# Keeping the residual as token rows: the norms behind the first FFN and the second out-projection done per chunk of 128 tokens

## The reference, cut to what matters

```python
def rmsnorm(x, g):
    y = xf * lax.rsqrt(jnp.mean(xf * xf, axis=-1, keepdims=True) + EPS)
    return (y * g.astype(F32)).astype(x.dtype)
...
x <- x + gate * RMSNorm_post(f(RMSNorm_pre(x) * (1 + scale) + shift))
```

## Time and profile before

| | us |
|---|---|
| median of 3 runs | 1950.3 (1949.1 to 1951.3) |
| the profiled execution, its own time | 1951.7 |
| its span in the profile | 1949.9 |
| PE busy | 1896.0 (97%) |
| VectorE busy | 987.0 (51%) |
| ScalarE busy | 666.7 (34%) |
| GpSimd busy | 191.5 (10%) |

### The profile page before, as it was taken

How to read it: one execution, slowest core, us unless ns; L and a number is a source line. 1 busy time by engine, 2 the same in 40 slices (tenths; PEclk the granted TensorE clock), 3 DMA queues, 4 the chain that set the end, 5 groups by cost and what they waited for, 6 DMA issues and landing times.

```text
span 1949.9 us, 29286 instructions
## 1 busy us (share of the span) xinstructions
PE 1896.0 (97%) x11961; PEld 1742.5 (89%) x11961; DVE 987.0 (51%) x1763; ACT 666.7 (34%) x869; POOL 191.5 (10%) x172
## 2 busy tenths in 40 slices
PE   6999999989999999999999999999999999999998
PEld 5768987759999999998999999998898998899987
DVE  5415446476553555558543343336367653355533
ACT  4323234343331333335422223224344432133312
POOL 3100001410000000141000000001240000000002
PEclk8999999999999999999999999999999999999999
DMA  9843103762213231344232221335753221323221
GB/s 276 337 173 98 55 28 116 243 203 65 78 54 96 74 86 51 89 134 157 84 103 67 92 79 38 101 110 186 246 130 87 78 73 54 97 65 86 65 86 55
DMA packets 243851, 214.36 MB, mean 110 GB/s; under 512 B 7804, under 2 KB 227188, under 8 KB 238644
## 3 DMA queue, kind: packets, MB, share of 16 engines
q1 hardware_dynamic: 234163, 193.45, 32.9%
q10 hardware_dynamic: 7504, 10.74, 1.6%
q0 software_dynamic: 2096, 8.94, 1.3%
HBM read 197.89 MB, written 11.02 MB: 107 GB/s over the span
## 4 chain that ended last, share of the span: by engine, by line
PE 83%; DVE 9%; issue 2%; DMA 2%; ACT 2%; POOL 1%; SPq 0%; DVEq 0%; POOLq 0%; ACTq 0%
PE PJ L2141 43%; PE PJ L2304 8%; PE PJ L2152 7%; PE AT L2610 4%; PE PJ L2610 3%; PE PJ L2275 2%; PE AT L2162 2%; PE AT L2491 1%; DVE uT L1406 1%; PE AT L2507 1%; DMA xT<-in_ada_w 1%; PE AT L2120 1%; PE PJ L2162 1%; PE AT L2504 1%; PE AT L2340 1%
## 5 line engine op out<-in xcount | busy, mean ns | idle before, releaser
L2141 PE MATMUL PJ<-h_both,w_high 128*128 128x320 f32 x3584 | 674.7, 310 | 0.3 <-DVE sq L1881 0.3
L2141 PEld LDWEIGHTS PJ<-h_both,w_high 128*128 128x128 f32 x3584 | 562.3, 188 | 3.5 <-issue 1.7
L1881 DVE SCALAR_TENSOR_TENSOR sq<-PJ,cols,sq 128x127 f32<-128x127 f32 (+2 forms) x504 | 189.1, 430 | 237.9 <-ACT sq L1216 226.9
L2141 PE MATMUL PJ<-h_both,w_low 128*128 128x320 f32 x1280 | 291.7, 309 | 0.0
L1469 DVE TENSOR_TENSOR w_low<-ring,w_high 128x2048 fp32r<-128x2048 f32 (+3 forms) x80 | 171.4, 2143 | 109.5 <-ACT w_high L872 109.4
L2141 PEld LDWEIGHTS PJ<-h_both,w_low 128*128 128x128 f32 x1280 | 214.0, 188 | 0.0
L872 ACT ACTIVATE w_high<-ring 128x2048 fp32r<-128x2048 f32 (+3 forms) x80 | 142.8, 1785 | 150.5 <-PE PJ L2141 51.6
L2304 PE MATMUL PJ<-w_high,h_both 128*128 128x256 f32 (+1 forms) x672 | 160.2, 329 | 0.0
L1483 DVE TENSOR_TENSOR ring_low<-ring,w_high 128x2048 fp32r<-128x2048 f32 x38 | 86.9, 2287 | 125.7 <-ACT w_high L889 124.7
L1216 ACT ACTIVATE sq<-PJ,cols 128x640 f32<-128x640 f32 x84 | 74.4, 886 | 191.5 <-PE PJ L2141 188.8
L638 POOL TENSOR_TENSOR sqsum<-sqsum,sq 128x320 f32<-128x320 f32 x42 | 80.9, 1926 | 539.1 <-issue 413.8
(11 more groups left out here) (319 smaller groups left out, 3120.0 us busy)
## 6 DMA issues: line engine op xcount, KB each, us to landing
ring<-in_ffn_w_up SPq DMA_DIRECT2D x88, 512.0 KB, 5.0
ring<-in_ret_w_in SPq DMA_DIRECT2D x24, 1024.0 KB, 7.7
hT<-in_ada_w SPq DMA_DIRECT2D x22, 1024.0 KB, 5.8
ring<-in_ret_w_out SPq DMA_DIRECT2D x14, 1024.0 KB, 5.7
ring<-in_ml_w_in SPq DMA_DIRECT2D x12, 1024.0 KB, 9.8
ring<-in_ffn_w_down SPq DMA_DIRECT2D x28, 384.0 KB, 3.8
turn<-in_ada_w SPq DMA_DIRECT2D x10, 1024.0 KB, 7.3
ring<-in_ffn_w_down SPq DMA_DIRECT2D x20, 512.0 KB, 4.4
```

The lines of the kernel that those rows point to most:

```text
L1881: ins = v.scalar_tensor_tensor(o, z, scalar, o, ALU.mult, ALU.add)
L2141: ins = pe.matmul(PJ[:, s, b, 0:HALF], w[:, at + k * step:at + k * step + P], x[:, k, b * HALF:(b + 1) * HALF], start=(k == 0 and n == 0), ...
```

## The change

1. The down projection of the first FFN takes the form of the last one: token chunks stationary, 512 weight columns moving. `turn_x` moves from the last down projection to the first, and from there on the residual stays as token rows `x_tok` to the end of the kernel. It is saved per chunk (five DMAs of GpSimd, `save_x(c)`) and read back into the same form. The units of the second column half in a part 1 come in the order tiles 4 to 7, 0 to 3, 8 to 11.
2. Layer 1's out-projection takes that form too: 8 units of 4 tiles by 512 columns (`out_unit`, `out_run`) in place of 16 half tiles, so that its weights are loaded and split once, not twice.
3. The norms of gaps 1 and 2 go per chunk, in an order common to ScalarE and VectorE, `END_STEPS`. A chunk has four steps: "y" (bank added to the first part's rows, its square summed, root), "x" (VectorE multiplies by the rows of post factors, then reciprocal, scaling and addition of the residual in two halves; ScalarE squares the new rows and takes the root), "s" (reciprocal, rows times the pre factors), "u" (after eight transposes on PE, `turn_scaled`, ScalarE copies the eight turned tiles with the shift as the high part and VectorE makes the low part). In gap 2 VectorE multiplies straight from the bank, and nothing is added. In gap 3 GpSimd still multiplies.
4. The last two units run interleaved by chunk with the turns behind them (`last_runs`, `TURN_BEHIND`), and the next sublayer starts with `lead_tokens` in place of `lead_pair`: four tiles on the first 256 tokens, with the turns of chunks 3 and 4 between them, then the same four tiles on the rest, 64 and 320 tokens a weight.
5. The factor rows of gaps 1, 2 and 3 are written to DRAM by GpSimd with element-wise DMAs and read back broadcast to all partitions (before: for gap 3 only). The memory for GpSimd's DMA descriptors is smaller (`dynamic_dma_scratch_size=2048`).
6. The statistics matmuls, the 128x320 reciprocals, GpSimd's sums and the feature-wise additions and splits of gaps 1 and 2 are gone.

```diff
-                      ((0, 0, 4), (0, 4, 4), (0, 8, 4), (1, 0, 4), (1, 4, 4), (1, 8, 4)))
-        LAST_RUNS = ((4, 0), (4, 1), (5, 0), (5, 1), (4, 2), (5, 2), (4, 3), (5, 3), (4, 4), (5, 4))
+                      ((0, 0, 4), (0, 4, 4), (0, 8, 4), (1, 4, 4), (1, 0, 4), (1, 8, 4)))
+        LAST_RUNS = ((0, 0), (0, 1), (1, 0), (1, 1), (0, 2), (1, 2), (0, 3), (1, 3), (0, 4), (1, 4))
+        TURN_BEHIND = {2: 0, 3: 1, 4: 2}
+        END_STEPS = (("y", 0), ("x", 0), ("y", 1), ("s", 0), ("x", 1), ("y", 2), ("s", 1), ("u", 0), ("x", 2), ("y", 3),
+                     ("s", 2), ("u", 1), ("x", 3), ("y", 4), ("s", 3), ("u", 2), ("x", 4), ("u", 3), ("s", 4), ("u", 4))
+        NEXT = (None, (1, 0), (1, 24))
+        RUNS_AT = (0, 0, 55, 90)
+        READ_AT = (0, 0, 20, 30)
+        ROWS_IN = (0, 96, 192, 256)
         TURNS_AT = (0, 1, 1, 1, 1, 1, 1, 1, 1, 2)
...
+            def write_rows(gap, kind, factors):
+
+                with nc.allow_non_contiguous_dma(reason="one factor a feature and group"):
+                    for grp in range(2):
+                        pool.dma_start(rows_dram[gap, kind, grp].rearrange("(k p) -> p k", p=P), factors[:, :, grp]
+                                       ).then_inc(row_out, 16)
+
+            def read_post(gap):
+
+                for grp in range(2):
+                    for nh in range(2):
+                        pool.dma_start(post_rows[grp][nh], rows_dram[gap, 0, grp:grp + 1, nh * WIDE:(nh + 1) * WIDE
+                                                                     ].to_broadcast([P, WIDE])).then_inc(row_in, 16)
+
+            def read_pre(gap):
+
+                for grp in range(2):
+                    pool.dma_start(pre_rows[grp], rows_dram[gap, 1, grp:grp + 1, :].to_broadcast([P, D_MODEL])
+                                   ).then_inc(row_in, 16)
+
+            def post_product(gap, nh, c):
...
+            def end_step(gap, kind, c, banks):
+
+                at = 10 * (gap - 1)
+                if kind == "y":
+                    if banks:
+                        a.wait_ge(run_done, RUNS_AT[gap + 1] - CH + c + 1)
+                        square_rows(gap, 1, c, banks[c])
+                    else:
+                        a.wait_ge(bank_read, READ_AT[gap] + 15 + c + 1)
+                        square_rows(gap, 1, c, y_tok[:, c, WIDE:2 * WIDE])
+                    a.wait_ge(y_squared, at + CH + c + 1)
+                    a.activation(end_rstd[:, c:c + 1], end_sums[:, 1, c:c + 1], ACT.Sqrt, scale=1.0 / D_MODEL,
+                                 bias=end_base[:, c:c + 1]).then_inc(y_std, 1)
+                elif kind == "x":
+                    a.wait_ge(x_new, CH * (gap - 1) + c + 1)
+                    link(a.activation(y_tok[:, c, :], x_tok[:, c, :], ACT.Square, accum_out=x_sum[:, c:c + 1]))
+                    a.activation(x_rstd[:, c:c + 1], x_sum[:, c:c + 1], ACT.Sqrt, scale=1.0 / D_MODEL, bias=eps[:, 0:1]
+                                 ).then_inc(x_std, 1)
+                elif kind == "u":
+                    of, sub = NEXT[gap]
+                    for h in range(2):
+                        a.wait_ge(xs_turned, at + 2 * c + h + 1)
+                        for k in range(4 * h, 4 * h + 4):
+                            ins = a.activation(u_high[:, k, c * P:(c + 1) * P], TURN_BANKS[h][:, (k % 4) * P:(k % 4 + 1) * P],
+                                               ACT.Identity, bias=mod[:, of, sub + k, min(c, 1):min(c, 1) + 1])
+                        ins.then_inc(uh_tok, 1)
...
+            def post_of_bank(gap, nh, c, bank):
+
+                v.wait_ge(y_squared, 10 * (gap - 1) + CH * nh + c + 1)
+                y = y_tok[:, c, nh * WIDE:(nh + 1) * WIDE]
+                v.tensor_tensor(y, bank, post_rows[min(c, 1)][nh], ALU.mult).then_inc(bank_read, 1)
+
+            def post_of_rows(nh, c):
+
+                v.wait_ge(y_squared, CH * nh + c + 1)
+                y = y_tok[:, c, nh * WIDE:(nh + 1) * WIDE]
+                v.tensor_tensor(y, y, post_rows[min(c, 1)][nh], ALU.mult).then_inc(t_ready, 1)
+
+            def end_step(gap, kind, c, banks):
+
+                at = 10 * (gap - 1)
+                if kind == "y":
+                    v.wait_ge(run_done, RUNS_AT[gap + 1] - CH + c + 1 if gap < 3 else RUNS_AT[3] + RUNS_AT[2] - CH + c + 1)
+                    if gap == 2:
+                        post_of_bank(2, 1, c, banks[c])
+                    else:
+                        y = y_tok[:, c, WIDE:2 * WIDE]
+                        v.tensor_tensor(y, banks[c], y, ALU.add).then_inc(bank_read, 1)
+                elif kind == "x":
+                    if gap == 1:
+                        post_of_rows(1, c)
+                    v.wait_ge(y_std, CH * (gap - 1) + c + 1)
+                    link(v.reciprocal(end_rstd[:, c:c + 1], end_rstd[:, c:c + 1]))
+                    for nh in range(2):
+                        part = slice(nh * WIDE, (nh + 1) * WIDE)
+                        if gap == 2:
+                            v.wait_ge(bank_read, READ_AT[2] + CH * nh + c + 1)
+                        else:
+                            v.wait_ge(t_ready, (0, 0, 0, 10)[gap] + CH * nh + c + 1)
+                        scaled = end_scaled[c] if gap == 3 and nh == 1 else y_tok[:, c, part]
+                        ins = v.scalar_tensor_tensor(y_tok[:, c, part] if gap == 3 else x_tok[:, c, part], scaled,
+                                                     end_rstd[:, c:c + 1], x_tok[:, c, part], ALU.mult, ALU.add)
+                        if gap == 3:
+                            ins.then_inc(end_out, 1)
+                    if gap < 3:
+                        ins.then_inc(x_new, 1)
+                elif kind == "s":
+                    v.wait_ge(x_std, CH * (gap - 1) + c + 1)
+                    link(v.reciprocal(x_rstd[:, c:c + 1], x_rstd[:, c:c + 1]))
+                    v.scalar_tensor_tensor(y_tok[:, c, :], x_tok[:, c, :], x_rstd[:, c:c + 1], pre_rows[min(c, 1)],
+                                           ALU.mult, ALU.mult).then_inc(xs_ready, 1)
+                else:
+                    of, sub = NEXT[gap]
+                    for h in range(2):
+                        v.wait_ge(uh_tok, at + 2 * c + h + 1)
+                        for k in range(4 * h, 4 * h + 4):
+                            here = slice(c * P, (c + 1) * P)
+                            ins = v.scalar_tensor_tensor(u_low[:, k, here], TURN_BANKS[h][:, (k % 4) * P:(k % 4 + 1) * P],
+                                                         mod[:, of, sub + k, min(c, 1):min(c, 1) + 1],
+                                                         u_high[:, k, here].bitcast(F32), ALU.add, ALU.subtract)
+                        ins.then_inc(ul_tok, 1)
...
+            def chunk_run(high, low, of_high, of_low, k0, nk, c, bank, first, last):
+
+                for k in range(nk):
+                    at = slice(k * WIDE, (k + 1) * WIDE)
+                    for n, (x, w) in enumerate(((of_high, high), (of_high, low), (of_low, high))):
+                        ins = pe.matmul(bank, x[:, k0 + k, c * P:(c + 1) * P], w[:, at],
+                                        start=(first and k == 0 and n == 0), stop=(last and k == nk - 1 and n == 2))
...
+            def turn_scaled(gap, c):
+
+                pe.wait_ge(xs_ready, CH * (gap - 1) + c + 1)
+                for h in range(2):
+                    if c == 0:
+                        pe.wait_ge(bank_read, READ_AT[gap] + (14 if gap == 1 else 5))
+                        if gap == 2:
+                            pe.wait_ge(y_squared, 10 + CH)
+                    else:
+                        pe.wait_ge(ul_tok, 10 * (gap - 1) + 2 * c - 1 + h)
+                    for k in range(4 * h, 4 * h + 4):
+                        ins = pe.transpose(TURN_BANKS[h][:, (k % 4) * P:(k % 4 + 1) * P], y_tok[:, c, k * P:(k + 1) * P], ident)
+                    ins.then_inc(xs_turned, 1)
+
+            def last_runs(gap, run):
+
+                for i, c in LAST_RUNS:
+                    ins = run(i, c)
+                    if i == 1:
+                        ins.then_inc(run_done, 1)
+                        if gap < 3 and c in TURN_BEHIND:
+                            turn_scaled(gap, TURN_BEHIND[c])
+
+            def lead_tokens(gap, highs, lows, ats, step):
+
+                read = READ_AT[gap] + (10 if gap == 1 else 0)
+                slots = [pj_slot(), pj_slot()]
+                outs = [PJ[:, slots[0], :, :], PJ[:, slots[1], :, :], AT[:, 0:2, :], AT[:, 2:4, :]]
+
+                def products(m, spans):
+
+                    w_of = (highs[m // 2], lows[m // 2])
+                    for k in range(KT):
+                        at = ats[m % 2] + k * step
+                        for n, (w, x) in enumerate(((w_of[0], u_high), (w_of[0], u_low), (w_of[1], u_high))):
+                            for b, lo, hi in spans:
+                                ins = pe.matmul(outs[m][:, b, lo - b * HALF:hi - b * HALF], w[:, at:at + P], x[:, k, lo:hi],
```

(93 more changed lines are left out.)

581 lines of the change are left out of this document (236 added, 345 removed).

## The result

The changed kernel takes 1967.5 us (median of 4 runs, 1965.85 to 1968.9) against 1950.8 of the kernel before on the same chip: ratio 1.0086, 95% interval 1.0069 to 1.0104. It is 16.7 us slower; the forecast was 7.3, and the range (to 1968.0) just holds it.

What follows compares the result with a forecast made beforehand. Bound by PE: matmuls, plus its waits for the norms' chain. Terms -2.4 + 3.7 + 3.4 + 2.6 = +7.3 on the profiled 1951.7 gave 1959.0, less 1.4: 1957.6 us; range 1943.5 to 1968.

Steps and rivals of the forecast that it cites:

- Down projections: Part 0 of the first down projection +2.5 to 73.0, of the last -4.9 to 68.1; sum -2.4 us.
- PE's work: Matmul work alone in the two norms: +1.6 us in gap 1, +2.5 in gap 2; 64-column product 0.107.
- The rival of hidden loads: Weight loads run beside matmuls, a 64-column product costs 0.040, 12.9 us less: 1944.7; chance 0.12.
- The norm's chain: Gaps 1 and 2: 8.3 us a chunk on VectorE and ScalarE against PE's 5.4; gaps +3.7 and +3.4.
- the six terms given for it: Per-chunk turn: VectorE 2.2, ScalarE 1.5, 1.05 and 2.1, VectorE's low parts 1.05, handovers 0.3; given as 8.3 us.
- The clock: Granted clock drops after PE's new waits of 5.2 and 4.6 us; 1.3 a gap, +2.6; from below 0.
- What costs nothing: Factor rows' DMAs, residual saves, smaller descriptor memory, weight splits and the out-projection's single weight read: no time charged.
- The prediction's own sign of being wrong: Wrong if pairs come 0.19 apart, the turn per chunk is under 7 us, or the wait is for GpSimd's DMA.
- The rival of late rows: GpSimd's 4-byte factor-row writes land late and every chunk waits: +5 to +20, 1962 to 1977; chance 0.08.
- Its bound: In the rival of late rows: chunks wait if the rows land over 12 us later than 10.4 says.
- the clock's share: The 1.3 us charged per gap for one drop of the granted clock behind PE's wait.
- the terms that the sum put at 7.3: Down projections -2.4, gap 1 +3.7, gap 2 +3.4, clock +2.6: +7.3 us in all.

Runs made afterwards that it cites:

- the wide lead: Changed kernel with pre rows read before gap 3's writes, and one 384-column product replacing each pair of 64 and 320: 1940.4 us, ratio 0.9948.
- the filler: 18 unread products of 512 columns in PE's wait ahead of the turn of chunk 4, added to the wide lead: 1936.6 us, ratio 0.9924.

## Why the prediction came out as it did

**Down projections: right.** 72.88 and 68.03 measured, 73.0 and 68.1 forecast; the sum -2.4 came as -2.6.

**PE's work: right.** The pair costs 0.258, 0.254 was forecast, so the 64-column product costs 0.112 and not the 0.040 of its columns. That the rest is its weight load is the prediction's reading; the runs show the price and not the reason. The rival of hidden loads at 0.040 is out. The Trainium skill's "TensorE: Matmul & The Clock Gate", "Back-to-back issue gap", gives some 81 ns for 128 columns; the trace does not agree, here half the columns take 112. That the pairs' 8.2 us a gap are hardly hidden is shown by the wide lead, 15.6 less for the two.

**The norm's chain: right in form, a little long.** A turn per chunk takes 7.8 where 8.3 was forecast (the six terms given for it add up to 8.2); the wait ahead of the turn of chunk 4 is 4.7 (5.2) and 4.1 (4.6), released by VectorE's scaling in both gaps. Gap 1 took 133.4 against 132.9 and the clock's 1.3.

**The clock: right in kind, too small.** It fell at the place named, to 0.60 and 0.72 over ten us. Charged was 1.3 a gap; the filler gives back 1.9. Not foreseen at all was that the level can stay down under a busy PE, as it did with the turn behind the fourth leading tile; the changed kernel's order happened to avoid it.

**What costs nothing: wrong, and this is the step that failed.** It said that the factor rows "go out by GpSimd DMAs and come back broadcast: 10.4 to land, then 4.3" and that they "are needed some 40 us after the previous work of that queue". The time to land was taken once, from a row of two writes. Four writes stand ahead of the read, and with the smaller descriptor memory each is issued some 10 us behind the one before: 43.3 us to the read and 8.1 for it, 51.9 after the first issue (the row with 4.3 is one read of 256 KB, this is two of 512). VectorE came to its wait about 40 after it. The prediction's own sign of being wrong, "if the wait is for a DMA of GpSimd's", came true for PE's largest wait, which was not the 5 us ahead of the turn of chunk 4 but 10.4 ahead of that of chunk 0. The rival of late rows, given 0.08, is what happened, in gap 2 only: in gap 1 the six writes went out from 435.8 on, hundreds of microseconds ahead. Its bound, "over 12 us later than 10.4", does not follow from the 40 us: those less 10.4 and 4.3 leave 25. With the order of two writes changed gap 2 is 163.6 long, where 164.9 was forecast with the clock's share, and the time 1956.0 against 1957.6. So of the 16.7 us, 11.5 are the late rows, and the other 5.2 are the terms that the sum put at 7.3. That these came so near is in part luck: the clock's share was too small and the norm's chain too long, and the two errors offset each other. And the range holds 1967.5 only because half of the late rows' rival was taken into it. The smaller descriptor memory was priced at nothing in the same step, "can only delay the issues of an engine that is busy 10% of the span", with its price, if there is one, left to that rival. It did delay them, and an engine that is idle was what the whole core waited for.

At the start of the kernel the smaller memory also spreads GpSimd's issues (the last at 26.7 instead of 10.1); no cost of it shows: the part up to the first FFN's down projection ends at 564.0, against 563.5 before and 564.3 with the larger memory, within what it varies from run to run.

## What to carry to other kernels

Before costing a queue's transfers at nothing, count those that stand ahead of the one that is needed, price the series and not one of it, and put what is wanted last behind what is wanted first; an idle engine's queue can be the longest chain. Put a wait right ahead of the step that needs what it waits for, not ahead of the whole series. Let the tokens that are ready early end on a bank's edge, so that the rest is one long product instead of a short and a long one with a weight load each. A wait of PE of a few microseconds also has a price behind it: 1.9 us a gap here, and 20 with pairs of 64 and 320 columns next. Read the granted clock of the stretch behind each such wait, try what is best to run there, and try filler in the wait.

## What the runs showed of the hardware

Pairs of 64 and 320 columns kept the level of the granted clock at which they began, at either level: 1.00 behind busy PE (12.40 us for 48 pairs), 0.50 behind waits of 1.8 and 3.0 us with a turn between (23.41), and there PE was busy for 46 us on end and was granted 0.50 all the time. Products of 384 columns in the same place had 1.00 again some 5 us after they began. A single reordering of two calls thus cost 40 us.

Writes of 1024 elements of 4 bytes each from GpSimd's queue were issued 10 to 13 us apart with `dynamic_dma_scratch_size` at 2048 (11.3, 10.7, 12.7, 9.9 and 12.0 for the six ahead of gap 1); with 4032 three were issued 0.9 us apart, and the fourth 20 us behind the first.
